# Query tiles 2 to 7 and twelve up tiles of the expert layer in three passes, with low parts made by GpSimd

## The reference, cut to what matters

```
q = (xt @ w_query).reshape(T, 8, 2, 128)
scores = einsum('thpc,hpnc->thpn', q, sub_keys)          # 16 sets of 128 scores per token
top_s, top_i = top_k(scores, 16)
cand = all 16 x 16 sums of each head; best = top_k(cand, 16)
gate = softmax(best)
y[t] = sum over the 128 chosen experts e: gate * gelu(x[t] . u[e]) * v[e]
```

## Time and profile before

| what | us |
|---|---|
| median of 3 runs | 3216.35 (3215.09 to 3220.65) |
| the profiled execution's own time | 3216.33 |
| its span, first to last instruction | 3214.5 |
| PE busy | 3080.9 |
| DVE busy | 1919.0 |
| ACT busy | 1290.4 |
| POOL busy | 1.8 |

### The profile page before, as it was taken

The page is one execution under the profiler, slowest core; times in us unless marked ns, Lnnn a source line. Parts: engine busy times, 40 slices in busy tenths (PEclk is TensorE's granted clock), DMA queues, the critical chain, the costliest instruction groups (busy, mean ns, idle before and its releaser), DMA issues.

```text
span 3214.5 us, 54764 instructions
## 1 busy us (share of the span) xinstructions
PE 3080.9 (96%) x20362; PEld 2643.1 (82%) x20362; DVE 1919.0 (60%) x3711; ACT 1290.4 (40%) x1988; POOL 1.8 (0%) x6
## 2 busy tenths in 40 slices
PE   8999899999999899989999999999998999999898
PEld 7688689898898768868989889887766979777697
DVE  3377974787647437796478764755534465543446
ACT  3321344444444332134444444444424444442444
POOL 0000000000000000000000000000000000000000
PEclk9999999999999999999999999998998999899899
DMA  5244155544555424415554455542233555223354
GB/s 192 92 158 145 67 195 183 193 158 144 187 182 195 145 92 158 148 65 194 183 195 157 144 186 182 208 179 110 92 131 131 183 184 194 96 92 133 135 186 148
DMA packets 68034, 493.66 MB, mean 154 GB/s; under 512 B 7576, under 2 KB 7584, under 8 KB 8352
## 3 DMA queue, kind: packets, MB, share of 16 engines
q1 hardware_dynamic: 67568, 490.42, 42.6%
q0 software_dynamic: 304, 1.06, 0.1%
HBM read 490.39 MB, written 1.06 MB: 153 GB/s over the span
## 4 chain that ended last, share of the span: by engine, by line
PE 88%; DVE 5%; issue 3%; ACT 2%; DVEq 1%; DMA 0%; SPq 0%; ACTq 0%
PE ps L647 9%; PE ps L649 9%; PE ps L648 9%; PE ps L233 9%; PE ps L617 8%; PE ps L618 7%; PE ps L619 7%; PE ps L699 5%; PE ps L243 2%; PE ps L269 2%; PE ps L1553 2%; PE ps L1580 2%; DVE hots L1270 2%; PE ps L959 2%; PE ps L295 1%
## 5 line engine op out<-in xcount | busy, mean ns | idle before, releaser
L761 DVE TENSOR_TENSOR ring_l<-ring,tile_h 128x1024 fp32r<-128x1024 f32 x632 | 745.7, 1222 | 665.4 <-ACT tile_h L717 665.3
L717 ACT ACTIVATE tile_h<-ring 128x1024 fp32r<-128x1024 f32 x632 | 633.5, 1051 | 548.2 <-PE ps L649 455.7
L617 PE MATMUL ps<-x_h,tile_h 128*128 128x256 f32 x2016 | 575.5, 285 | 0.8 <-DVE ring_l L761 0.8
L618 PE MATMUL ps<-x_l,tile_h 128*128 128x256 f32 x2016 | 570.0, 283 | 0.0
L619 PE MATMUL ps<-x_h,ring_l 128*128 128x256 f32 x2016 | 569.9, 283 | 0.0
L617 PEld LDWEIGHTS ps<-x_h,tile_h 128*128 128x128 f32 x2016 | 386.4, 192 | 1.8 <-issue 1.6
L618 PEld LDWEIGHTS ps<-x_l,tile_h 128*128 128x128 f32 x2016 | 386.5, 192 | 0.2
L619 PEld LDWEIGHTS ps<-x_h,ring_l 128*128 128x128 f32 x2016 | 386.3, 192 | 0.0
L721 ACT ACTIVATE arena<-ps 128x512 f32 (+1 forms) x160 | 95.5, 597 | 466.6 <-PE ps L619 345.5
L647 PE MATMUL ps<-tile_h,w_even 128*128 128x512 f32 x640 | 252.7, 395 | 15.7 <-DVE w_even L783 15.7
L233 PE MATMUL ps<-xT,ring 128*128 128x256 f32 x1216 | 265.1, 379 | 0.0
(11 more groups left out here) (303 smaller groups left out, 4906.8 us busy)
## 6 DMA issues: line engine op xcount, KB each, us to landing
ring<-stream SPq DMA_DIRECT2D x464, 1024.0 KB, 4.8
cs<-consts SPq DMA_DIRECT2D x1, 1712.5 KB, 8.5
x<-x_in SPq DMA_DIRECT2D x1, 1024.0 KB, 5.0
arena<-scratch POOLq DMA_DIRECT2D x1, 1024.0 KB, 7.8
out<-x SPq DMA_DIRECT2D x2, 512.0 KB, 2.7
tab<-table SPq DMA_DIRECT2D x1, 1.0 KB, 8.4
scratch<-arena POOLq DMA_DIRECT2D x1, 12.0 KB, 4.9
```

Source lines behind the costliest of these rows:

```text
L617: nc.tensor.matmul(out, uh[:, c, f], x_h[:, c, :], start=(c == 0), stop=False)
L618: nc.tensor.matmul(out, uh[:, c, f], x_l[:, c, :], start=False, stop=False)
L717: nc.scalar.activation(tile_h[:, j % 2, n], slot(k + j)[:, n], ACT.Copy).then_inc(hi_ready, 1)
L761: nc.vector.tensor_tensor(low_of(k + j)[:, n], slot(k + j)[:, n], tile_h[:, j % 2, n].bitcast(F32), ALU.subtract).then_inc(lo_ready, 1)
```

## The change

Query tiles 2 to 7 and up tiles 0 to 11, 18 tiles a layer (`AHEAD`), become three-pass products. Their high parts go into `early_h`, three buffers, of which two lie on `tile_h` and one on the last four rows of `hbuf`, unused at that time. GpSimd makes `x_l` and the low parts, in halves, in their slots. The keys move to another place in memory. PE takes the key scores of heads 0, 1 and 2 directly behind their own query tile, those of heads 3 to 7 one tile later. ACT makes `x_h` directly behind the layer norm and the high part of query tile 2 ahead of `queries_out(0)`; high parts follow ahead of each later step; the exps stand behind the tenth gelu (index 9). DVE no longer makes `x_l` ahead of the first down block. The last four up tiles stay plain.

```diff
...
         assert at[0] <= GATES
-        keys = room(TILE, GATES + BLK * 512)
+        keys = room(TILE, GATES + BLK * 512 + 2 * TILE + 2 * KC * SEQ)
...
         hot_rows = sem("hot_rows")
+        eh_ready, el_ready = sem("eh_ready"), sem("el_ready")
+        FIRST_WQ = 2
+        AHEAD = 8 - FIRST_WQ + EARLY
+        early_h = [nc.alloc_sbuf_tensor_at(f"early_h{b}", [P, TILE], F32R,
+                                           offset=arena_at + 4 * (GATES + BLK * 512 + (b - 1) * TILE)) for b in range(3)]
+
+        def early_tile(n):
+            return (A_WQ + FIRST_WQ + n) if n < 8 - FIRST_WQ else (A_EXP + n - (8 - FIRST_WQ))
...
                 .then_inc(xl_ready, 1)
+
+        def pe_early(pe, l, n, bank):
+            k = early_tile(n)
+            wh, wl = tile_chunks(early_h[n % 3][:, :]), tile_chunks(low_of(k))
+            for fb in range(2):
+                out, f = ps[bank][:, fb * SEQ:(fb + 1) * SEQ], slice(fb * P, (fb + 1) * P)
+                for c in range(KC):
+                    if c % 4 == 0 and fb == 0:
+                        pe.wait_ge(el_ready, l * (2 * AHEAD) + (2 * n + c // 4 + 1))
+                    nc.tensor.matmul(out, wh[:, c, f], x_h[:, c, :], start=(c == 0), stop=False)
+                    nc.tensor.matmul(out, wh[:, c, f], x_l[:, c, :], start=False, stop=False)
+                    last = nc.tensor.matmul(out, wl[:, c, f], x_h[:, c, :], start=False, stop=(c == KC - 1))
+            last.then_inc(tile_done, 1)
+
+        def act_early_high(act, l, n):
+            k = early_tile(n)
+            arrived(act, 1, l, k)
+            if n >= 3:
+                finished(act, 1, l, early_tile(n - 3))
+            for hf in range(2):
+                part = slice(1024 * hf, 1024 * hf + 1024)
+                nc.scalar.activation(early_h[n % 3][:, part], slot(k)[:, part], ACT.Copy).then_inc(eh_ready, 1)
+
+        def pool_early_lows(pool, l):
+            pool.wait_ge(xh_ready, 2 * l + 2)
+            nc.gpsimd.tensor_tensor(x_l[:, :, :], xT[:, :, :], x_h[:, :, :].bitcast(F32), ALU.subtract)\
+                .then_inc(xl_ready, 1)
+            for n in range(AHEAD):
+                k = early_tile(n)
+                for hf in range(2):
+                    part = slice(1024 * hf, 1024 * hf + 1024)
+                    pool.wait_ge(eh_ready, l * (2 * AHEAD) + (2 * n + hf + 1))
+                    nc.gpsimd.tensor_tensor(low_of(k)[:, part], slot(k)[:, part], early_h[n % 3][:, part].bitcast(F32),
+                                            ALU.subtract).then_inc(el_ready, 1)
...
             for h in range(8):
-                arrived(pe, 1, l, A_WQ + h)
+                if h == FIRST_WQ:
+                    pe.wait_ge(xl_ready, 2 * l + 2)
                 if h >= 2:
                     pe.wait_ge(wq_ev, l * 8 + (h - 1))
-                up = up_features(chunks(A_WQ + h), xT, 4 + h % 2) if h else \
-                    up_as_turned(pe, 2 * l + 1, chunks(A_WQ), 4, norm_and_keys_read)
-                up.then_inc(tile_done, 1)
-                if h:
+                if h >= FIRST_WQ:
+                    pe_early(pe, l, h - FIRST_WQ, 4 + h % 2)
+                else:
+                    arrived(pe, 1, l, A_WQ + h)
+                    up = up_features(chunks(A_WQ + h), xT, 4 + h % 2) if h else \
+                        up_as_turned(pe, 2 * l + 1, chunks(A_WQ), 4, norm_and_keys_read)
+                    up.then_inc(tile_done, 1)
+                if h < 3:
+                    key_scores(h)
+                elif h > 3:
                     key_scores(h - 1)
-            def plain_up(i, j):
-                k = A_EXP + j
-                arrived(pe, 1, l, k, i)
-                pe.wait_ge(u_act, g + 4 * i + (j + 1))
-                up_features(chunks(k), xT, 4 + j % 2).then_inc(tile_done, 1)
-
-            with pe.Fori(0, EARLY // 4) as i:
-                pe.wait_ge(wq_ev, l * 8 + 8)
-                for j in range(4):
-                    plain_up(i, j)
+            pe.wait_ge(wq_ev, l * 8 + 8)
+            for j in range(EARLY):
+                pe.wait_ge(u_act, g + (j + 1))
+                pe_early(pe, l, 8 - FIRST_WQ + j, 4 + j % 2)
             pe.wait_ge(key_ev, l * 8 + 8)
...
-            queries_out(0)
-            for h in range(8):
-                if h < 7:
-                    queries_out(h + 1)
+            def scores_out(h):
                 act.wait_ge(key_mm, l * 8 + (h + 1))
                                      ACT.Copy).then_inc(key_ev, 1)
+
+            act.wait_ge(xt_ready, 4 * KC * l + 4 * KC)
             act_split_x(act)
-            with act.Fori(0, 2) as i:
-                for j in range(4):
-                    act_apply(act, 1, l, A_EXP, i, j, ACT.Gelu)
-            for tt in range(TT):
-                act.wait_ge(g_diff, l * TT + (tt + 1))
-                nc.scalar.activation(gexp[:, tt, :, :], gexp[:, tt, :, :], ACT.Exp).then_inc(g_exp, 1)
-            for j in range(EARLY - 8):
-                act_apply(act, 1, l, A_EXP, 2, j, ACT.Gelu)
+            act_early_high(act, l, 0)
+            for h in range(8):
+                if h >= 1:
+                    act_early_high(act, l, h)
+                queries_out(h)
+                if h < 3:
+                    scores_out(h)
+                elif h > 3:
+                    scores_out(h - 1)
+            scores_out(7)
+            for j in range(EARLY):
+                if 8 + j < AHEAD:
+                    act_early_high(act, l, 8 + j)
+                act_apply(act, 1, l, A_EXP, j // 4, j % 4, ACT.Gelu)
+                if j == EARLY - 3:
+                    for tt in range(TT):
+                        act.wait_ge(g_diff, l * TT + (tt + 1))
+                        nc.scalar.activation(gexp[:, tt, :, :], gexp[:, tt, :, :], ACT.Exp).then_inc(g_exp, 1)
             for tt in range(TT):
...
             k, g, s = A_EXP, l * PAIRS, l * SPLIT_A + PROJ_A
-            dve_split_x(dve, 2 * l + 1)
...
             band = bass.AP(tensor=scratch.tensor, offset=0, ap=[[1, P], [384, 8], [1, 256]])
+            for l in range(LAYERS):
+                pool_early_lows(pool, l)
             pool.wait_ge(tile_done, (LAYERS - 1) * A_TILES + (A_EXP + 7 * BLK + 1))
```

## The result

The changed kernel takes 3236.77 us in the median (3236.25 to 3237.78 in four runs), the kernel before on the same chip 3215.72 us. The ratio is **1.0054, with an interval of 1.0042 to 1.0066**: about 17 us slower by the ratio, 21 by the two medians, where 8 us faster was forecast. The time lies inside the range given, on the side of rival B, whose own time was 3235; that is no merit of the forecast, whose likeliest case alone had a range that ended at 3214. The profiled execution has a span of 3234.7 us against 3214.5 before.

What follows compares the result with a forecast made beforehand. The prediction took PE to bound the early tiles and DVE the gate stage; 3.7 + 0.4 = 4.1 us a layer, 8.2 in two, off 3216.33 gave 3208.1 us, with a range from 3203 to 3238.

Steps and rivals of the forecast that it cites:

- rival B: DVE's selection: two-input operations wait for GpSimd's pieces, 19 us in eight heads; +9.4 us a layer, 3235 us; chance 0.27.
- likeliest case: The forecast itself, whole kernel: 4.1 us a layer faster, 3208.1 us, own range 3203 to 3214; chance 0.44.
- Three passes, 5.76 a tile: PE's 18 early tiles a layer: 5.76 us each against 6.91, 20.7 us less if nothing waits.
- The pause and the clock behind it: PE behind query tile 0: waits about 5.1 us for ACT's copy, then loses 2.2 us to a slow clock.
- DVE's start: Start of DVE's selection on the scores of head 0: at 188.7 us, 0.8 us earlier than 189.50.
- GpSimd's pieces: GpSimd's half-tile subtractions, 36 a layer: 2.29 us each, `x_l` twice that, hidden behind PE's tiles.
- rival D: GpSimd too slow for PE's early tiles: 3.5 us a piece, +7 us a layer, 3230 us; chance 0.11.
- `x_l` off DVE, 0.4 us a layer: Product L780 behind the gates: starts 0.4 us earlier, not 2.2, since it also needs ACT's last gate row.
- The exp, moved later, 9.1 us behind PE: DVE's choice waits for ACT's exp, goes on at 298.5, ends at 316.7; one-hot work at 319.8, 3.7 us earlier.
- GpSimd beside DVE: Both engines during the selection: lower bound zero, nothing charged to the end, as DVE has 12.5 us spare.

Runs made afterwards that it cites:

- order: Changed kernel with ACT's copies of query tile 0 and head 0's scores ahead of the high part of query tile 2: 3232.05 us, 1.0031 of the kernel before.
- write_only: Changed kernel with each GpSimd subtraction replaced by two writes of zero, low parts left out: 3213.29 us, 0.9971 of the kernel before.
- exp_early: Changed kernel with the two exps behind the seventh gelu in place of the tenth: 3245.26 us, 1.0074 of the kernel before.
- psum_all: Changed kernel with one operand of DVE's selection operations, candidate sums included, in PSUM (two small subtractions excepted): 3208.59 us, 0.9961 of the kernel before.
- one_input: Changed kernel with GpSimd copying the high part in place of each subtraction, low parts left out: 3213.24 us, 0.9972 of the kernel before.

## Why the prediction was wrong, by its own steps

*Three passes, 5.76 a tile.* Right: ACT's gelus of the up tiles come at 249.48, 255.24, 261.00. PE's end was forecast at 307.6 and is 307.04.

*The pause and the clock behind it.* Right in kind: 4.54 us for 5.1. Tile 2 landed at 183.11, as taken from the earlier trace rows. The granted clock fell to the same level as in the earlier trace rows, 0.50, but for a shorter time: it is 0.50 from the end of the pause at 185.6 to about 188.7 us and then 1.00 (0.63 is the mean of the row above), where the earlier trace rows has 0.50 for 4.4 us. The key scores started 1.86 us ahead of tile 1, for 0.91 where the clock is 1.00, and tile 1 took 7.69 us, for the 7.07 of the run order: 1.6 us lost, for the 2.2 taken, which is half of the 4.4 us of the earlier trace rows, where 10 matmuls ran, and 20 in the next 4.3. With the shorter pause, PE was 1.0 us ahead of the sum at the end of tile 1 (195.2 for 196.2).

*DVE's start.* 188.40 for 188.7: right.

*GpSimd's pieces.* They took 2.43 us for the 2.29 taken, and `x_l` 4.61 for twice 2.29. Hidden as said; rival D didn't happen.

*`x_l` off DVE, 0.4 us a layer.* This gain didn't arrive. The product, now L788, starts 65.4 us behind the one-hot work (332.28 to 397.71); before it was 64.75. The saved 2.28 us are followed by a DVE wait of 2.10 for ACT's last gate row, and that row comes later than before against the one-hot work. PE enters the gates out of a pause; whether the clock behind it is the reason was not tested.

*The exp, moved later, 9.1 us behind PE.* Its sum was right for ACT and never came into play: ACT's exps ran at 297.47, so DVE could have gone on at about 298, and it arrived at 310.64. Write_only, which has the same order, shows the step as predicted: DVE on at 297.78 for 298.5, one-hot work at 319.43 for 319.8.

**The step that failed is "GpSimd beside DVE", costed at zero.** The text put it as "I charge nothing to the end, since DVE has 298.5 - 286.0 = 12.5 us of spare time". It measures 15.5 us in the heads and 9.5 in the first half of the tokens, 25.0 a layer: twice the spare time. The slack took about 12 of it, the rest moved the one-hot work from 319.4 (write_only) to 332.3. Against before that is +8.8, with 0.7 in the gate stage +9.5 in layer 0 and +9.3 in layer 1: 18.7 of the 20.2 us between the spans. Of the rest, 0.9 us lies between the first product of layer 0 and query tile 0 of layer 1 and 0.5 behind the stage of layer 1; their cause stays open.

Rival B had the mechanism, the place and nearly the price: 19 us in the heads (15.5), one-hot work at 333.3 (332.28), the kernel at 3235 (median 3236.77). It came that close partly by luck, since it took 3.5 us too much in the heads and 2.5 too little in the first half of the tokens (24.5 for 27.0). It had 0.27 and the forecast 0.44 because of one argument, that DVE keeps its turn through a run of operations and only the start of a run waits. The eight operations of L1291 refute that: spread over two pairs of pieces they lose 6.5 us, and in exp_early, over six gapless pieces of 2.5 us, the eight take 2.0 us each in the mean, about one to a piece. The argument for the lower bound was the wrong comparison as well: ACT reading the tiles that DVE works on the earlier trace rows says nothing of GpSimd. What the runs show of the conflict: the sums go from 412 to 1371 ns with two SBUF inputs, and take 419 with one of them in PSUM and 413 beside a GpSimd that only writes. I had put it into one rival of three, weighed down by a guess of mine that no row supported.

## What to carry to other kernels

Before work is put on an idle GpSimd, count what VectorE does in the same stretch by the number of SBUF inputs, and charge each two-input instruction there a wait of up to one whole GpSimd instruction (412 ns became up to 2.62 us here, beside pieces of 2.43); slack covers it only if it is larger than that sum. Casts and integer operations with one input are to be looked at too (below). Where one operand could live in PSUM, the wait went (L1291: 619 to 414 ns) for next to nothing (a cast that writes there took 428 ns for 294) or for a small copy (174 ns per head here), and an offload that lost 0.5% became one that gained 0.4%. After such a change look again at every place where a third engine waits for the slowed one: an earlier exp was worth 5.5 us a layer in one version and cost 4 in the other.

## What the runs showed of the hardware that was not expected

- The conflict is one-sided in its cost. A pair of GpSimd pieces takes 4.66 to 4.82 us in psum_all, where hardly an operation of DVE contends, and 4.67 to 5.18 in the changed kernel, while DVE's 0.41 us operation takes 1.37 in the mean and up to 2.62.
- Operations of DVE with one input waited too, in two forms: the cast of 256 integers to fp32 took 2.38 us for 0.29 beside the subtraction and 598 to 648 ns in the mean beside plain writes, and an integer `tensor_scalar` 2.45 us for 0.22. The groups of searches with one fp32 input (275 to 420 ns) kept their means to within 2 ns in all these runs. A cast that writes to PSUM takes 410 to 428 ns and didn't wait beside the subtractions.
- A copy of 1024 fp32 elements per partition takes GpSimd 1.05 us in the median (one_input), a write of zeros 0.95 (write_only), the subtraction with two inputs 2.43 in the mean.
